# A two-layer diffusion backbone: the dense expert products in three float32r products, with the remainder subtracted in PSUM

## The reference

```python
sc, pos = lax.top_k(cand, PEER_TOPK)
eidx = jnp.take_along_axis(cidx, pos, axis=-1)
gw = jax.nn.softmax(sc, axis=-1)
a = jnp.einsum('thkd,td->thk', u_tab[eidx], hb)
w = (jax.nn.gelu(a.astype(jnp.float32), approximate=False) * gw).astype(hb.dtype)
return jnp.einsum('thk,thkd->td', w, v_tab[eidx])
```

## Time and profile before

| | |
|---|---|
| median of three runs | 4995.86 us |
| the profiled execution, its own time | 4959.93 us |
| its span | 4958.0 us |
| instructions | 60450 |
| TensorE busy | 84%, weight loads 66% |
| VectorE busy | 63% |
| ScalarE busy | 27% |
| GpSimd busy | 28% |
| mean granted TensorE clock | 0.91 of full speed |
| DMA traffic over the span | 253 GB/s |

### The profile page before, as it was taken

How to read it: one execution, slowest core, us unless ns; L and a number is a source line. 1 busy time by engine, 2 the same in 40 slices (tenths; PEclk the granted TensorE clock), 3 DMA queues, 4 the chain that set the end, 5 groups by cost and what they waited for, 6 DMA issues and landing times. The chain is left out here.

```text
span 4958.0 us, 60450 instructions
## 1 busy us (share of the span) xinstructions
PE 4174.8 (84%) x22612; PEld 3269.4 (66%) x22612; DVE 3115.2 (63%) x6389; ACT 1342.8 (27%) x2581; POOL 1364.4 (28%) x1291
## 2 busy tenths in 40 slices
PE   7977798979999998689988797757889998787786
PEld 5864686866666665566666583545778888666675
DVE  3135874249988778567676723583279867456565
ACT  2115433123454555000000112422234565300000
POOL 0000000004333445546666300000024334344341
PEclk9989898989999998799999897868999999898897
DMA  4120103149888999999999700251279999899995
GB/s 171 60 78 13 60 6 93 43 164 356 327 297 289 413 396 413 389 404 404 404 404 404 273 19 20 48 120 60 94 279 343 337 357 413 334 405 402 402 403 226
DMA packets 469174, 1254.74 MB, mean 253 GB/s; under 512 B 52094, under 2 KB 191092, under 8 KB 463252
## 3 DMA queue, kind: packets, MB, share of 16 engines
q0 software_dynamic: 184320, 671.17, 35.0%
q1 hardware_dynamic: 279032, 570.96, 31.5%
q10 hardware_dynamic: 5532, 8.74, 0.5%
HBM read 1147.46 MB, written 103.25 MB: 252 GB/s over the span
## 5 line engine op out<-in xcount | busy, mean ns | idle before, releaser
L1962 PE MATMUL banks<-acts_in,v_rows 128*128 128x256 f32 (+2 forms) x5120 | 1160.9, 390 | 246.8 <-DMA v_rows<-peer_v 238.2
L1962 PEld LDWEIGHTS banks<-acts_in,v_rows 128*128 128x128 f32 x5120 | 913.7, 196 | 493.7 <-DMA v_rows<-peer_v 258.5
L1578 PE MATMUL banks<-h_dense,u_t 128*128 128x384 f32 (+1 forms) x4096 | 1207.6, 439 | 0.0
L1552 POOL DMA_INDIRECT rows<-peer_u,expert x640 | 632.8, 989 | 1648.9 <-DVE weight L1855 809.2
L1578 PEld LDWEIGHTS banks<-h_dense,u_t 128*128 128x128 f32 x4096 | 750.7, 193 | 250.2 <-issue 7.6
L1940 POOL DMA_INDIRECT v_fetched<-peer_v,expert x640 | 718.4, 1123 | 703.4 <-DVE banks L2006 318.7
L1855 DVE CUSTOM_DVE_ANT_0 rows<-rows,banks 128x1024 f32<-128x1024 f32 x640 | 765.7, 1211 | 195.3 <-DMA rows<-peer_u,expert 128.0
L2006 DVE SCALAR_TENSOR_TENSOR row_sums<-v_fetched,weight,row_sums 128x1024 f32<-128x1024 f32 x378 | 472.9, 1280 | 112.7 <-DMA v_fetched<-peer_v,expert 111.9
L1637 ACT COPY u_t<-banks 128x512 f32<-128x512 f32 x512 | 300.0, 586 | 294.1 <-PE banks L1569 291.5
L1983 DVE TENSOR_TENSOR acts_in<-acts_in,gates 128x384 f32<-128x384 f32 (+1 forms) x256 | 125.0, 488 | 400.1 <-DMA acts_in<-activations 399.8
L1569 PE MATMUL banks<-ident,u_raw 128*128 128x128 f32 x2048 | 315.3, 278 | 64.4 <-DMA u_raw<-peer_u 64.2
(11 more groups left out here) (464 smaller groups left out, 5572.3 us busy)
## 6 DMA issues: line engine op xcount, KB each, us to landing
u_raw<-peer_u SPq DMA_DIRECT2D x256, 512.0 KB, 7.7
v_rows<-peer_v SPq DMA_DIRECT2D x256, 512.0 KB, 18.3
gate_table<-part SPq DMA_DIRECT2D x20, 2048.0 KB, 11.8
activations<-acts SPq DMA_DIRECT2D x128, 192.0 KB, 5.6
gates<-gate_table SPq DMA_DIRECT2D x8, 3072.0 KB, 27.2
acts_in<-activations SPq DMA_DIRECT2D x128, 192.0 KB, 22.2
peer_wq_in<-peer_wq SPq DMA_DIRECT2D x16, 1024.0 KB, 5.4
ada_ring<-ada_w SPq DMA_DIRECT2D x32, 512.0 KB, 4.5
```

What stands on the lines that cost most here:

```text
L1552: pool.indirect_dma_start(out=ring[:, s % U_RING, :], out_offset=None, in_=rows_of_u, in_offset=bass.IndirectOffsetOnAxis(ap=expert[:, t, ...
L1578: last = nc.tensor.matmul(out, u_t[:, i % 2, k * P:(k + 1) * P], h[:, k], start=(k == 0), stop=(k == DK - 1))
L1962: last = nc.tensor.matmul(ps[:, lo:hi], v[:, j % V_ROWS, m * P:(m + 1) * P], acts[:, j % V_ROWS, lo - m * ND:hi - m * ND], start=(j == 0 a ...
```

## The change

The u rows are now split as h is: `u_hi`, the turned rows rounded to float32r, and `u_lo`, the remainder. A dense activation is `u_hi` by `hi`, `u_hi` by `lo` and `u_lo` by `hi`, three float32r products instead of a float32 one. ScalarE rounds a turned half out of PSUM (`rounded`), TensorE multiplies `u_hi` with the negative identity onto the same bank (`remainder`, 512 columns), so the bank holds the remainder, and ScalarE copies this out (`rest_out`). The transposes run two half tiles ahead. `h_dense` and its sum on VectorE go.

```diff
+            def turn_ahead(s):
+                i, half = divmod(s, 2)
+                if half == 0:
+                    pe.wait_ge(u_loaded[i % U_ROWS], 16 * (i // U_ROWS + 1))
+                if s >= 2:
+                    pe.wait_ge(ulo_ready, s - 1)
+                for k in range(HALF):
+                    c = (half * HALF + k) * P
+                    last = nc.tensor.matmul(ps[:, TURN + c:TURN + c + P], u_raw[:, i % U_ROWS, c:c + P], g.ident[:],
+                                            start=(k == 0), stop=False, is_transpose=True, skip_group_check=True)
+                last.then_inc(turned, 1)
+            def remainder(s):
+                pe.wait_ge(uhi_ready, s + 1)
...
+                nc.tensor.matmul(ps[:, TURN + c:TURN + c + BANK], minus_r[:], u_hi[:, i % 2, c:c + BANK],
+                                 start=False, stop=True, skip_group_check=True).then_inc(rest_ready, 1)
+            def products_hi(s):
+                pe.wait_ge(uhi_ready, s + 1)
...
+                for k in range(half * HALF, (half + 1) * HALF):
+                    for n, part_h in enumerate((hi, lo)):
+                        nc.tensor.matmul(out, u_hi[:, i % 2, k * P:(k + 1) * P], part_h[:, k, 0:ND],
+                                         start=(k == 0 and n == 0), stop=False)
+            def products_lo(s):
+                pe.wait_ge(ulo_ready, s + 1)
...
+                for k in range(half * HALF, (half + 1) * HALF):
+                    last = nc.tensor.matmul(out, u_lo[:, i % 2, k * P:(k + 1) * P], hi[:, k, 0:ND], start=False,
+                                            stop=(k == DK - 1))
...
+            for s in range(2 * KEYS if SPLIT else 0):
+                products_hi(s)
+                if s + 2 < 2 * KEYS:
+                    turn_ahead(s + 2)
+                if s + 1 < 2 * KEYS:
+                    remainder(s + 1)
+                products_lo(s)
+                if s % 2 == 0:
+                    gates(due(s // 2))
...
+            def rounded(s):
+                act.wait_ge(turned, s + 1)
...
+                nc.scalar.copy(u_hi[:, i % 2, c:c + BANK], ps[:, TURN + c:TURN + c + BANK]).then_inc(uhi_ready, 1)
+            def rest_out(s):
+                act.wait_ge(rest_ready, s + 1)
...
+                nc.scalar.copy(u_lo[:, i % 2, c:c + BANK], ps[:, TURN + c:TURN + c + BANK]).then_inc(ulo_ready, 1)
...
             for i in range(KEYS):
                 if i:
                     gelu(i - 1)
                 if i + 1 < KEYS:
-                    turned_out(i + 1, 0)
+                    rounded(2 * i + 2) if SPLIT else turned_out(i + 1, 0)
+                if SPLIT:
+                    rest_out(2 * i + 1)
                 keep(due(i))
                 if i + 1 < KEYS:
-                    turned_out(i + 1, 1)
+                    if SPLIT:
+                        rounded(2 * i + 3)
+                        rest_out(2 * i + 2)
...
-            nc.vector.tensor_tensor(h[:], hi[:, :, 0:ND].bitcast(F32), lo[:, :, 0:ND].bitcast(F32), ALU.add)\
-                .then_inc(h_ready, 1)
```

More of the change, by code:

```diff
@@ L1481, in stage_peer_activate @@
             "own_a")
+        uhi_ready, rest_ready, ulo_ready = a.sem("uhi_ready", "rest_ready", "ulo_ready")
         u_loaded = [a.sem(f"u_loaded{r}") for r in range(U_ROWS)]
@@ L1581, in products @@
                     last.then_inc(acted, 1)
+            def turn_ahead(s):
[10 more added lines that the diff above has]
+            def remainder(s):
+                i, half = divmod(s, 2)
+                pe.wait_ge(uhi_ready, s + 1)
+                c = half * BANK
+                nc.tensor.matmul(ps[:, TURN + c:TURN + c + BANK], minus_r[:], u_hi[:, i % 2, c:c + BANK],
+                                 start=False, stop=True, skip_group_check=True).then_inc(rest_ready, 1)
+            def products_hi(s):
+                i, half = divmod(s, 2)
+                pe.wait_ge(uhi_ready, s + 1)
+                if half == 0 and i >= 2:
+                    pe.wait_ge(gelued, i - 1)
+                out = ps[:, ACTS + i % 2 * BANK:ACTS + i % 2 * BANK + ND]
+                for k in range(half * HALF, (half + 1) * HALF):
[3 more added lines that the diff above has]
+            def products_lo(s):
+                i, half = divmod(s, 2)
+                pe.wait_ge(ulo_ready, s + 1)
+                out = ps[:, ACTS + i % 2 * BANK:ACTS + i % 2 * BANK + ND]
+                for k in range(half * HALF, (half + 1) * HALF):
+                    last = nc.tensor.matmul(out, u_lo[:, i % 2, k * P:(k + 1) * P], hi[:, k, 0:ND], start=False,
+                                            stop=(k == DK - 1))
+                if half:
+                    last.then_inc(acted, 1)
             def turn_h(j):
@@ L1613, in gates @@
                     last.then_inc(multiplied, 1)
-            pe.wait_ge(ident_ready, 1)
+            pe.wait_ge(ident_ready, 2 if SPLIT else 1)
             turn_h(0)
-            turn(0, 0)
-            turn(0, 1)
-            pe.wait_ge(h_ready, 1)
-            for i in range(KEYS):
+            if SPLIT:
+                turn_ahead(0)
+                turn_ahead(1)
+                remainder(0)
+            else:
+                turn(0, 0)
+                turn(0, 1)
+                pe.wait_ge(h_ready, 1)
+            for s in range(2 * KEYS if SPLIT else 0):
[7 more added lines that the diff above has]
+                    gates(due(s // 2))
+            for i in range(0 if SPLIT else KEYS):
                 if i + 1 < KEYS:
@@ L1687, in _ @@
             nc.scalar.copy(ident_r[:], g.ident[:]).then_inc(ident_ready, 1)
-            turned_out(0, 0)
-            turned_out(0, 1)
+            if SPLIT:
+                nc.scalar.activation(minus_r[:], g.ident[:], ACT.Copy, scale=-1.0).then_inc(ident_ready, 1)
+                rounded(0)
+                rounded(1)
+                rest_out(0)
+            else:
+                turned_out(0, 0)
+                turned_out(0, 1)
             for i in range(KEYS):
```

15 lines of the change are left out of this document (13 added, 2 removed).

## The result

The changed kernel takes **5009.48 us** (median of 7 runs, 5007.74 to 5023.23); the kernel before, timed beside it, 4994.56 (7 runs, 4981.61 to 4999.61). The ratio is **1.0056, with an interval from 1.0039 to 1.0074**: slower by 0.56%, some 28 us, where I forecast 10 less. In this first set the two medians lie only 15 us apart and the means 22. Two repetitions on other chips gave 1.0053 both times, with medians 28 and 27 us apart, so I go by 27 to 28 us.

The account below looks back on a forecast made before the run. VectorE was taken to end layer 0's stage and TensorE layer 1's. Layer 0's -19 us and layer 1's +9 summed to -10: 4950 us for the profiled execution, 4986 from the median, range 4946 to 5022.

Parts of the forecast that it names:

- the prices: TensorE's time per key without a quad: 5.55 us for 6.04 in layer 0, 4.15 for 4.33 in layer 1.
- The chain in layer 1: Layer 1 quad keys: ScalarE's second copy delays the relu, so TensorE's gates wait 0.56 us; 5.59 us for 5.22.
- the restart's 0.08: Layer 1 quad keys: 0.08 us more for the product behind the wait, making +0.37 into +0.45.
- the waits of 47.6 us stay as they are: Layer 1: TensorE's 20 waits for U rows, 47.6 us in all, would not change.
- TensorE keeps what it wins up to key 67: Layer 0, from key 35 to the turning of h: 32 x 0.49 = 15.7 us won.
- the -19 us: Layer 0's stage 19 us shorter, through VectorE's two waits for the turning of h; bounds nothing and 34 us.
- a layer 0 that ends with TensorE: Layer 0's stage: named as a sign that would show the prediction wrong, since VectorE was to end it.
- layer 1's +9: Layer 1's stage: +23 us from 51 quad keys, -14 from the other 77; bounds -23 and +17.
- a spread of 12 us about 4986: Whole kernel: the forecast's own case, chance 0.50, with 0.15 of it below 4981 and 0.02 above 5011.
- Late landings eat layer 0's gain: Rival, layer 0: VectorE resumes earlier but its rows land as late as before; +9, 5005 us; chance 0.13.
- Slower, by the clock: Rival, layer 1's quad keys: granted clock falls behind 51 holes, 1.6 us each; +49, 5045 us; chance 0.10.
- ScalarE's copy stays covered: Rival, layer 1: ScalarE's second copy causes no wait; -19 - 23 = -42, 4954 us; chance 0.22.

Follow-up runs that it names:

- after_hold: Changed kernel plus 14 small Exp holds put on ScalarE in layer 1 keys without a quad; 1.0065 to the kernel before.
- after_rows4: Changed kernel with four rows in u_raw instead of three; 0.9928 to the kernel before.
- split_l0: Changed kernel with the float32r form in layer 0 alone, layer 1 old; 0.9996 to the kernel before.
- relu_late_rows4: Changed kernel with four u_raw rows and ScalarE's relu behind the copies; 0.9886 to the kernel before.
- ring3_load_first: Changed kernel, three TURN banks, transposes three half tiles ahead, late relu, four rows, SP's load ahead of its gelu wait; 0.9879 to the kernel before.
- before_hold: Kernel before plus 14 small Exp holds put on ScalarE in layer 1 keys without a quad; 1.0014 to the kernel before.
- split_l1: Changed kernel with the float32r form in layer 1 alone, layer 0 old; 1.0062 to the kernel before.
- relu_late: Changed kernel with ScalarE's relu moved behind the remainder's copy and the rounding; 0.9987 to the kernel before.
- ring3: Changed kernel with late relu, three TURN banks, one gates bank, transposes three half tiles ahead, four u_raw rows; 0.9891 to the kernel before, 4912.46 us.
- before_load_first: Kernel before, three rows, with SP's load of a U row ahead of its wait for the gelu; 0.9885 to the kernel before, 4925.88 us.
- the second group: Four kernels on one chip: changed kernel with four rows (0.9928), deeper pipeline with three (1.0095), holds put into old (1.0014) and changed kernel (1.0065).

## Why the prediction was wrong

**Right: the prices.** 5.53 and 4.17 us for keys of 5.55 and 4.15. Products of 384 columns start 0.173 us apart, between the bounds as chosen (0.175), and weight loads lie beside them: L1617's loads take 193 ns each, more than lies between two starts.

**Right: the chain in layer 1.** The gates wait for the relu 52 times, 0.4 us each; quad keys take 5.70 us for 5.67 (5.59 and the restart's 0.08). Taking this wait out makes them 5.07.

**Wrong: "the waits of 47.6 us stay as they are", and with it layer 0's "TensorE keeps what it wins up to key 67".** I looked only at layer 1, and only at whether the waits grow there. In layer 1 they did not (37.1 us). In layer 0, for which I had no term, they stood between TensorE and the -19 us. The cleanest pair are two profiles without holds: after_hold, with three rows, has a layer 0 of 936.1 us and VectorE's longer wait for the turning of h at 23.5; after_rows4 has 919.8 and 13.9. **The -19 is nearly there once rows come in time**: with early loads in both forms it is 938.2 to 922.4, -16. As the change was made it was -5 without holds (941.1 to 936.1), and with them -7 in the profiles of one chip (951.5 to 944.3) and -2 by the ratio of split_l0. Rows in time are not enough in every form: relu_late_rows4 and ring3_load_first, both with holds, have 931.9 and 933.4 us, and there VectorE stands idle for 6.9 and 10.3 us at the end, waiting for TensorE's last quads. TensorE's waits for U rows in layer 0, in before_hold:

```profile
PE banks L1570 <- DMA u_raw<-peer_u: 15.2, 10, 2.7
```

and in after_hold:

```profile
PE banks L1599 <- DMA u_raw<-peer_u: 30.6, 10, 4.7
```

after_rows4 has none.

Why rows are waited for twice as long in layer 0 stays open. From load to use it is no shorter than before in keys without a quad: 10.99 us before, 11.33 in after_hold. Of the 15.4 us more, 10.6 come behind 1500 us, where the DMA engines are full (a share of 0.98 from 1500 to 2000 us in after_hold, 386 GB/s); that the same rows are asked of them at a faster pace would fit, and wasn't tested. What the old form's layer 0 gains by early loads is not clear either: its 938.2 us were measured with holds, and stand against 941.2 without them and 951.5 with them (split_l1).

One sign of the prediction came true against it: a layer 0 that ends with TensorE. In the three profiles of the changed kernel VectorE stands idle for 6.2, 10.4 and 5.3 us before its last instruction there; in after_hold, without holds in that layer, for 0.6, as in before.

**Missing: ScalarE's holds.** No term and no rival had them, since the one trace that I had showed none. I did write that the transposes run two halves ahead, and did not ask what has to happen between: a half now passes TensorE and ScalarE twice before its bank is free. The waits show it: in layer 0 the transposes wait 20.5 us on the remainder's copy and 11.0 on "issue" in the changed kernel, and 4.4 and 0 in after_hold. What this costs can be estimated. Without holds the changed kernel would be 4988.1 (after_hold) less 24.3 (the put-in holds) = 4963.8 us, against 4955.1 of before on that chip: 9 us, a ratio of 1.0018. The changed kernel itself never met a chip without holds, and three ratios with their intervals are in this sum. With holds it is 27 us, so **the holds' share is about 18 us, by some 12 either way**. By the stages it all falls in layer 1: the new form is 10 us longer there without holds (next paragraph) and 32 with them. The holds cost the old form something as well, or so it seems: its layer 0 takes 951.5 us in split_l1 and 941 without holds, and its medians are 4955 without, 4970 to 4995 elsewhere; but chips may differ in more than this.

The sum, then: forecast -19 + 9 = -10. Without holds -5 in layer 0, and 723.1 - 687.6 less 25.6 for the 14 put-in holds = +10 in layer 1 make +5, beside the 9 from the medians. Holds bring 18 more. So layer 1's +9 was right as long as ScalarE isn't held; the first error is a term of layer 0 set to zero that was 14, the second a mechanism that was not in the list. (A slip in the chances: half of a spread of 12 us about 4986 puts 0.17 below 4981, not 0.15, and 0.01 above 5011, not 0.02.)

**The rivals.** "Late landings eat layer 0's gain" (0.13, 5005 us) came nearest in time, and by luck: the late rows are TensorE's and not VectorE's, and the larger loss is layer 1's. "Slower, by the clock" did not happen in its place. In before the granted clock was 0.61 from 1615 to 1619 us, behind a wait of 1.97 us for a U row, and in the changed kernel 0.50 behind the 3.58 us of key 8. Behind the holes of 0.3 to 0.4 us from 4109 to 4121 it was 1.00, and the key stayed at 5.70; behind the wait of 1.61 us in after_hold it was 1.00 too (3775 to 3786). Over layer 1's stage the granted clock was 0.95, for 0.96 before. "ScalarE's copy stays covered" was wrong, by the 52 waits.

**On equal supply** the float32r form is still slower: 0.9923 against 0.9885, 19 us, on two chips that both have holds. In the two profiles that is -16 in layer 0 and +34 in layer 1, and layer 1's transposes wait 20.9 us on the remainder's copy and 10.7 on "issue". With relu_late too it is level (0.9891), not ahead, though its keys of layer 1 are 0.16 us shorter. ring3 has 654.5 us there, the old form with early loads 655.4: by then VectorE, which waits 57.2 us for its own rows in before_load_first and only 8.1 us for the last gelu, nearly ends that stage too. So the shorter key has little left to shorten; this is read from the waits and wasn't tested.

## What to carry to other kernels

A faster engine step is worth what the supply behind it and the slack around it allow: before pricing a product, measure how long a load's slot lies free until the load is issued. Here moving one load ahead of an unrelated wait was worth 1.15%, twice what the change lost. The form that sends each piece twice through ScalarE exposed TensorE to ScalarE's pauses (a hold of 2.8 us cost it 1.83, the old form nothing), not only to its mean duration, and 5 of the 20 profiles do not show a pause that wasn't put in at all. That more distance in the loop would cure it is not shown: with equal supply a third bank brought nothing here.

## What the runs showed of the hardware

- **ScalarE pauses with no releaser in the profile.** In 14 of the 18 profiles of my experiments, and in the changed kernel's first, ScalarE started instructions up to 10 us after everything that the profile shows them waiting for was done, nearly always roundings and copies that wait for TensorE. It went by chips: every profile of four groups had such pauses, the four of the second group and that of before had none. The line is sharp, and "remote" is not the whole of it: in those five profiles neither ScalarE nor VectorE has a single row of "remote" or "issue" in the two stages, in the other 15 ScalarE has 26 to 86 us of the first and 43 to 110 of the second, and VectorE 10 to 35 of both. Some of the "issue" may be ordinary waits whose releaser the profile missed. They come in the old form too; ScalarE's waits in before_load_first:

```profile
ACT part L1661 <- remote: 33.0, 8, 5.3
ACT u_t L1637 <- remote: 24.3, 16, 10.0
```

  Its "remote" and "issue" rows sum to 148 us, as much as the changed kernel's 150. What makes the pauses stays open.
- **A table load took 1.28 us, a switch there and back 2.8 us** with the small Exp between, from 3775.85 to 3778.66 in after_hold. Both loads and the Exp of 0.22 us fit into the 2.8.
- **In the changed kernel PSUM took an unfinished transpose as the start of a sum.** Four transposes with `stop=False`, then a float32r product with the negative identity onto the same bank, left the remainder there for the price of one 512-column product. I had it at 0.233 us; from its start to the next product's it took 0.31 (4252.07 to 4252.38 in the changed kernel), and the four transposes before it 0.35 instead of 0.44, so the sum for a key came out right although both terms were off.
